# Moving the start of the activation tensors by less than one 64-byte line

## The reference

```
x = x + 0.5*ml[2]*swiglu(modulate(rms_norm(x, norm1_g), ml[0], ml[1]), ffn1_w_in, ffn1_w_out)
cx = cx + 0.5*mc[2]*swiglu(modulate(rms_norm(cx, norm1_g), mc[0], mc[1]), ffn1_w_in, ffn1_w_out)
bg, cg, vc, q, k, v, gt = split(hx @ w_in)               # first block, hx = modulated norm of x
x = x + ml[5] * (g_conv*(y_conv @ w_bc) + g_attn*(o @ w_ba)) @ w_out
x = x + 0.5*ml[8]*swiglu(modulate(rms_norm(x, norm3_g), ml[6], ml[7]), ffn2_w_in, ffn2_w_out)
u = rmsnorm(x) @ w_in_ab;  y = concat(mlstm(...), stick_breaking(...)) @ w_out_ab
u = rmsnorm(x) @ w_in_c;   y = (pooled @ pool_w * scale * silu(z)) @ w_out_c
```

## Time and profile before

| | |
|---|---|
| runs | 1336.4, 1337.29, 1349.08 us |
| profiled execution, its span | 1343.2 us, 5.9 us above the median of the runs |
| PE busy | 98% of the span |
| DVE, ACT, POOL busy | 67%, 48%, 2% |
| DMA engines' share of the weight queue | 53.8% |
| TensorE's granted clock, mean | 0.991 of full |

### The profile page before, as it was taken

The page is one execution under the profiler, slowest core; times in us unless marked ns, Lnnn a source line. Parts: engine busy times, 40 slices in busy tenths (PEclk is TensorE's granted clock), DMA queues, the critical chain, the costliest instruction groups (busy, mean ns, idle before and its releaser), DMA issues. The chain is left out here.

```text
span 1343.2 us, 23450 instructions
## 1 busy us (share of the span) xinstructions
PE 1312.1 (98%) x9320; PEld 1214.2 (90%) x9320; DVE 903.8 (67%) x1461; ACT 645.0 (48%) x1026; POOL 27.3 (2%) x27
## 2 busy tenths in 40 slices
PE   5999999999999999999999999999999999999998
PEld 3688888888889999999999999998999999999998
DVE  3577875556558497755775555678887666689873
ACT  4432222222336335545554445566666766556553
POOL 0000000000020000000000000200000000100000
PEclk6999999999999999999999999999999999999999
DMA  8746556464554345444545655565556445536660
GB/s 304 262 161 200 190 188 217 160 233 163 190 178 142 111 137 162 137 147 135 180 145 186 199 172 171 164 188 154 155 149 188 142 141 185 162 110 205 207 202 32
DMA packets 201484, 230.20 MB, mean 171 GB/s; under 512 B 7072, under 2 KB 191648, under 8 KB 201376
## 3 DMA queue, kind: packets, MB, share of 16 engines
q1 hardware_dynamic: 201088, 228.42, 53.8%
q10 hardware_dynamic: 288, 0.28, 0.1%
HBM read 227.63 MB, written 1.05 MB: 170 GB/s over the span
## 5 line engine op out<-in xcount | busy, mean ns | idle before, releaser
L1048 PE MATMUL P<-XHB,WH 128*128 128x256 f32 (+1 forms) x1808 | 556.0, 308 | 7.6 <-DVE XLB L1707 3.7
L1049 PE MATMUL P<-XLB,WH 128*128 128x256 f32 (+1 forms) x1808 | 546.0, 302 | 0.0
L1050 PE MATMUL P<-XHB,WL 128*128 128x256 f32 (+1 forms) x1808 | 545.9, 302 | 0.0
L1911 DVE TENSOR_TENSOR WL<-W,WH 128x1024 fp32r<-128x1024 f32 x358 | 431.9, 1225 | 89.9 <-ACT WH L1490 89.7
L1490 ACT ACTIVATE WH<-W 128x1024 fp32r<-128x1024 f32 x358 | 368.8, 1041 | 251.2 <-PE P L1050 162.3
L1048 PEld LDWEIGHTS P<-XHB,WH 128*128 128x128 f32 x1808 | 340.9, 189 | 28.1 <-issue 7.3
L1050 PEld LDWEIGHTS P<-XHB,WL 128*128 128x128 f32 x1808 | 342.2, 189 | 14.8
L1049 PEld LDWEIGHTS P<-XLB,WH 128*128 128x128 f32 x1808 | 340.6, 188 | 15.3 <-issue 0.5
L1048 PE MATMUL P<-GH,WH 128*128 128x256 f32 (+1 forms) x372 | 122.1, 328 | 0.0
L1049 PE MATMUL P<-GL,WH 128*128 128x256 f32 (+1 forms) x372 | 121.5, 327 | 0.0
L1050 PE MATMUL P<-GH,WL 128*128 128x256 f32 (+1 forms) x372 | 121.5, 327 | 0.0
(11 more groups left out here) (314 smaller groups left out, 1791.4 us busy)
## 6 DMA issues: line engine op xcount, KB each, us to landing
W<-in_ffn_w_in SPq DMA_DIRECT2D x88, 512.0 KB, 4.8
W<-in_w_in_ab SPq DMA_DIRECT2D x72, 512.0 KB, 4.7
W<-in_w_modt SPq DMA_DIRECT2D x56, 512.0 KB, 3.8
W<-in_w_in SPq DMA_DIRECT2D x52, 512.0 KB, 3.7
W<-in_ffn_w_out SPq DMA_DIRECT2D x40, 512.0 KB, 4.6
W<-in_w_in_c SPq DMA_DIRECT2D x32, 512.0 KB, 4.4
W<-in_w_mod SPq DMA_DIRECT2D x16, 512.0 KB, 7.4
W<-in_w_out_ab SPq DMA_DIRECT2D x16, 512.0 KB, 4.3
```

Source lines behind the costliest of these rows:

```text
L1048: pe.matmul(o, h[:, k, c], xh[:, kk, a:b], start=kk == 0, stop=False)
L1049: pe.matmul(o, h[:, k, c], xl[:, kk, a:b], start=False, stop=False)
L1050: mm = pe.matmul(o, l[:, k, c], xh[:, kk, a:b], start=False, stop=kk == gm.nk - 1)
L1911: dve.tensor_tensor(l, a, h.bitcast(F32), ALU.subtract).then_inc(S["wl"], 1)
```

## The change

The number of free elements in front of the activation tensors is changed. Weights, order, waits and instructions are the same.

```
-        XHB = sbuf(ctx, "XHB", [128, 4096 + 48], F32R)
-        XLB = sbuf(ctx, "XLB", [128, 4096 + 80], F32R)
-        X1H, XH = (XHB[:, a:a + 4096].rearrange("p (k t) -> p k t", k=8) for a in (0, 48))
-        X1L, XL = (XLB[:, a:a + 4096].rearrange("p (k t) -> p k t", k=8) for a in (80, 0))
+        XHB = sbuf(ctx, "XHB", [128, 4096 + 56], F32R)
+        XLB = sbuf(ctx, "XLB", [128, 4096 + 72], F32R)
+        X1H, XH = (XHB[:, a:a + 4096].rearrange("p (k t) -> p k t", k=8) for a in (0, 56))
+        X1L, XL = (XLB[:, a:a + 4096].rearrange("p (k t) -> p k t", k=8) for a in (72, 0))
...
-            sbuf(st, "PAD3", [128, 64])
+            sbuf(st, "PAD3", [128, 60])
             YH, YL = sbuf(st, "YH", [128, 8, T], F32R), sbuf(st, "YL", [128, 8, T], F32R)
...
-            sbuf(st, "PAD5", [128, 64])
+            sbuf(st, "PAD5", [128, 68])
             GH[2], GL[2] = sbuf(st, "GH2", [128, 12, T], F32R), sbuf(st, "GL2", [128, 12, T], F32R)
...
-            sbuf(st, "PAD6", [128, 64])
+            sbuf(st, "PAD6", [128, 56])
             ZH, ZL = sbuf(st, "ZH", [128, 16, T], F32R), sbuf(st, "ZL", [128, 16, T], F32R)
...
-            sbuf(st, "PAD7", [128, 64])
+            sbuf(st, "PAD7", [128, 66])
             RH, RL = sbuf(st, "RH", [128, 16, T], F32R), sbuf(st, "RL", [128, 16, T], F32R)
```

## The result

The changed kernel takes 1356.96 us in the median of 7 runs (1355.67 to 1358.44); the kernel before, run beside it, 1343.12 us (7 runs, 1336.4 to 1350.0). The ratio is **1.0121**, 95% interval 1.0086 to 1.0155: slower by 1.2%. Not only the median moved. The runs of before spread over 13.6 us, those of after over 2.8 us.

The account below looks back on a forecast made before the run. TensorE, busy 98% of the span, was taken to bound the kernel. The terms summed to 0 us, so the forecast was the median, 1338 us, own range 1321 to 1350, 8-in-10 range 1316 to 1366.

Parts of the forecast that it names:

- a rival's 1363: Slower time predicted if moving reads pay for starting inside a line, the smaller of two such prices; chance 0.14.
- What bounds it, and what could change: TensorE, busy 98%, bounds the kernel; only its distance between matmuls counts, and other engines cost 0.
- Where the tensors land: Starts round to 32 bytes: `YH` to `OL` stay at 192, `ZH` goes to 160, other moved tensors to 224; 6312 matmuls concerned.
- I take 0 ns: Price of a 32-byte start inside a line, for each of 6312 256-column matmuls on TensorE: none.
- I take the same two spacings: `XH`, moved from 192 to 224, was to keep steps of 113.3 and about 117.8 ns.
- all long: Edge case: 2750 short matmuls on TensorE take the long spacing, 12 us more; upper end 1350 us.
- The sign of being wrong: In TensorE's moved groups, a single new duration replacing both 276 and 281 ns would refute the forecast.
- slower rival: Moving reads of 6312 matmuls pay for starts inside a line; 283 ns or more; 1363 or 1382 us; chance 0.26.
- 224 lies on the good side: For `XH`, 224 and 288 lie farther from offset 0 than 192 and 320, taken as favourable; no size given.
- The row of `PT`: Eight plain float32 products inside a line take 1.89 us, as with `SQ` on a line: start costs nothing there.
- Spread of the runs as the mixture of spacings: Three runs differ by 12.7 us, about 2800 matmuls of 4.5 ns, so probably by their mixture of TensorE spacings.
- faster rival: Half a line separates clashing loading and moving reads on TensorE, ending the long spacing: 1321 us, floor 1294; chance 0.20.

Follow-up runs that it names:

- Experiment 4: Against the kernel before, eight free elements ahead of `WH` move weights and all tensors behind by 32 bytes, distances kept; 1340.5 us, ratio 1.0019.
- experiment 3: Against the kernel before, only `XH` and `XL` moved, to 256 bytes past the weights modulo 512, on a 64-byte line; 1355.3 us, ratio 1.0123.
- Experiment 9: The kernel before, unchanged, run and profiled once more against itself; 1337.5 us, ratio 0.9969.
- experiment 1: Against the kernel before, only `XH` and `XL` moved, from 192 to 224 bytes past the weights modulo 512; 1351.0 us, ratio 1.0089.

## Why the prediction was right or wrong

**The range held, the likeliest case did not.** Against the 1338 us forecast and the 1337.29 us then shown, the measured ratio makes 1353.5, inside 1316 to 1366; the measured 1356.96 us is inside too. That is partly luck: the range reached up to 1366 to take in a rival's 1363, and the loss fell between forecast and rival by a mechanism that neither had. The forecast itself was "within 1%, the two spacings remain". The measured ratio is 1.2% slower, with an interval that begins at 0.9%, so the time misses it by little; the trace misses it clearly, for on `XH` the two spacings didn't remain.

- **What bounds it, and what could change.** Right. Only TensorE's spacing moved; the other engines' rows stayed within 3 ns, and the run with `XH` alone and the run with the pads alone add up to the whole within their intervals.
- **Where the tensors land.** Right as far as the trace shows it: `YL` behind `PAD3` kept its 279 ns, `ZL`, `PL` and `WL,RH` behind the other pads changed. `GL` can't tell: it had 281 ns before and has 281 after, though its mean step in the second feed-forward went from 117.8 to 118.3 ns.
- **The step that failed: "I take 0 ns", "I take the same two spacings".** At 224 there is one main spacing of 118.3 ns. The kernel before had on `XH` a mixture of 0.6 long and 0.4 short, 116.0 ns by the prediction's own reading, so the term is 2.3 ns on 4320 matmuls, 9.9 us; `PH` adds 192 x 5.0 = 1.0 us and `RH` 384 x 3.4 = 1.3 us (twelve steps of `RH` in 1.40 us in the kernel after, below, against 113.3). That is 12.2 us beside 12.4 us more of busy time and 10.4 us more of span. The fit is less close than it looks: `ZH`, whose row rose from 278 to 280 ns, isn't in it and adds about 1 us. In effect the case "all long", 12 us, came true, which I had only used as an edge of the forecast's own range. A sum of 0 us would need a step that does not depend on the place; with the same instructions it was 113.3, 118.3 or 120 ns, as the two operands lay to each other.

```profile
1323.79 0.28 PE L1055 MATMUL P<-WL,RH 128*128 128x256 f32 x1
...
1325.19 0.28 PE L1055 MATMUL P<-WL,RH 128*128 128x256 f32 x1
```

- **The sign of being wrong** that the prediction named, a single new duration in place of both old ones, came in part: `XLB` has one main duration, 281 ns, but that of the old long spacing. The slower rival's sign, 283 ns or more, didn't come.
- **The slower rival had the sign and not the mechanism.** It let the moving read pay for its start inside a line. Experiment 4 puts every `float32r` operand inside a line and keeps 113.3 ns; experiment 3 puts all of them on lines and loses 1.2%. Its prices were both too high. The 1363 us is one step to the spacing of distance 0, 3562 x 2.2 + 2750 x 6.7 ns = 26 us. The 1382 us, the bound from above on the price of 32 bytes, takes 45 us for a whole extra line in each of the 6312 matmuls; that term was the author's assumption, and no run shows it. What the runs showed in its place is 12.4 us over 6312 matmuls, 2.0 ns each, and in experiment 4 steps of 113.3 ns with every start inside a line. What is lost is the possibility of the short spacing.
- **"224 lies on the good side".** Wrong: 256, the farthest from 0, is as bad as 0. The reasoning by nearness had nothing behind it but two points. Nor are 192 and 320 alike for being equally far from 0: `XH`'s mean step is 115.9 ns at the one and 117.4 at the other.
- **The row of `PT`**, 1.89 us for eight as with `SQ`, couldn't decide, as noted then: it spoke of a start inside a line and was right on that, but that was not the question.
- **Spread of the runs as the mixture of spacings.** Experiment 9 shows it for 5.8 us between two executions. The kernel after, in which the drawing is gone for most matmuls and the runs lie within 2.8 us, fits.
- **A reading that was too simple:** a mean of 279 ns isn't always the same mixture, nor a mixture at all. `XLB` has 279 ns with a mean step of 115.9 ns in the kernel before and of 117.4 with `XH` at 320. In line 1055 it is the long spacing itself, as here in the run with `XH` at 448, where the twelve rows show eleven steps in 1.29 us, 117 ns:

```profile
1309.81 0.28 PE L1055 MATMUL P<-WL,RH 128*128 128x256 f32 x1
...
1311.10 0.28 PE L1054 MATMUL P<-WH,RH 128*128 128x256 f32 x1
```

```profile
L1055 PE MATMUL P<-WL,RH 128*128 128x256 f32 x128 | 35.7, 279 | 0.0
```

For the working this touches 480 matmuls, under 1 us.

**Open.** Why, of the distances tried, only the odd multiples of 64 bytes have stretches of the short spacing, why it is rarer at 64 and 320, what picks it at a break, and why 196 is worse than 224. The runs show which distances do what, and that the spacing can change at a break or from one execution to the next with the code unchanged (852 and 885 matmuls in the same 100 us, experiment 9). The faster rival's clash between the weight load and the moving read was the author's guess; no row shows one, nor what the loading takes from a running read.

## What to carry to other kernels

In a `float32r` stream like this one, where each matmul of 256 columns has its own weight load, try the activation 192 or 448 bytes from the weight tiles modulo 512, exactly: the mean steps there were 115.9 and 116.3 ns, and one element off, at 196, it was 120.2 ns, no better than the 119.8 ns at 0 and 256. 64 and 320 were less good, 117.4 ns, and with 512 columns distance 0 was the better one, 226.7 ns against 233. What counted for a shift of 32 bytes is the distance between the two operands: 113.3 ns when both moved (experiment 4), 118.3 ns when `XH` and `XL` alone did (experiment 1). So check the real addresses: rounding to 32 bytes left `YH` at 192 where `PAD3` says 176. And read the distance between starts in several executions: a tuned kernel may hold two steady spacings, and then one profile is one draw.

## What the runs showed that I had not expected

- 4 bytes from the good place turn 113.3 or 117.8 ns into 120 ns, and 1343.5 us into 1360.1 us, while 32 bytes give 118.3 ns.
- The same code at the same addresses ran 852 or 885 matmuls between 700 and 800 us in two executions: one steady spacing per stretch, not noise around a mean.
- The slower layout is the steadier one: 2.8 us between its fastest and slowest run against 13.6 us, and against 6.7 us in the calmest set of runs of the kernel before.
- Tensors that nobody moved changed their spacing when `XH` moved: `GL` has 277 ns with `XH` at 208 and 281 with it at 200.
